# A first projection started by halves of the features, and identity products in TensorE's pauses

## The chip, the cores and the metric

One core of one Trainium2 chip. The time is device microseconds (us) for one execution of the whole program; of the kernel before there are three timed runs and one execution under the profiler.

## The reference

One step of a hybrid backbone with two layers, for 128 context tokens and 256 latent tokens of 1024 features, all in float32. Layer 0 mixes tokens by attention, layer 1 by a pooling over windows; each is followed by a mixture of 32 experts (two per token). Every sub-layer starts from a root-mean-square norm that is scaled and shifted by vectors made of the conditioning. Cut to what the change touches:

```python
def ada_modulation(cond, w, b):
    m = jax.nn.silu(cond) @ w + b            # 1024 -> 6 * 1024, per layer
    m = m.reshape(cond.shape[0], 1, N_MOD, D_MODEL)
    return tuple(m[:, :, i] for i in range(N_MOD))

def modulate(x, g, shift, scale):
    return rms_norm(x, g) * (1.0 + scale) + shift

for l in range(DEPTH):
    sh1, sc1, g1, sh2, sc2, g2 = ada_modulation(cond, ada_w[l], ada_b[l])
    h = modulate(x, norm_mix_g[l], sh1, sc1)
    m = attention(h @ w_qkv) @ w_o           # layer 0; pooling in layer 1
    x = x + g1 * m
    h = modulate(x, norm_ffn_g[l], sh2, sc2)
    x = x + g2 * hierarchical_moe(h, ...)
```

So the first product with `w_qkv` (1024 x 1536) needs `sh1` and `sc1`, which come from the first 2048 columns of `ada_w`.

## The kernel before

The program is written out by hand: each engine has its own list of instructions, in order, with waits on semaphores. Features lie on the 128 partitions in KD = 8 blocks k; tokens lie along the free axis, in three tiles of 128 (tile 0 is the context; `QTILES` = 1, 2, 0 is their order).

**The opening.** SyncE issues nearly all loads, in one order. `ada_w` comes in 24 chunks of 512 columns (2 MB each, `load_ada`, L409 to L411) into five places that are used in turn (`ADA_AT`); a chunk whose place was used before waits until TensorE has multiplied the earlier one (semaphore `ada_mm`). Chunks 0 and 1 hold the shift `sh1`, chunks 2 and 3 the scale `sc1`; the even one is for features 0 to 511, the odd one for 512 to 1023. The order of the loads is: constants, the tokens, chunks 0 to 3, two thirds of `w_qkv` (`load_qkv`, 2 MB each), chunk 4, the last third, chunks 5 and up.

TensorE (L1355 on) first makes the normed and turned tokens: 24 products of the tokens with `dg`, the identity scaled by the reciprocal root mean square (L1396), that VectorE copies to `hT` (`turned`, L908). Then, for chunks 0 to 3, `ada(i)` (L1374, eight products of 512 columns with 32 rows of output, four of them side by side in the array), with the transposes of the raw tokens between (`raw`, L1409; ScalarE copies them to `xT`, L694). `SETS` says which chunks share one bank: 0 to 3, 4 to 9, 10 to 23. When a set is complete, ScalarE copies it (`set_copy`, L689), `vectors` turns it into feature order (L1385), VectorE adds the bias, adds 1 and multiplies the gain (`modulation`, `scales`, L931 to L938), and scales and shifts `hT` block by block (L947, 16 operations). Only then the projection starts (L1449): nine groups g (three token tiles by three thirds of `w_qkv`), eight products each, into banks 5 to 7 in turn; between the groups stand `ada(4)` to `ada(11)` and the transposes for attention (`turn`, L1435). The other chunks are multiplied during attention (L1487 is its first product).

A product of float32 shows as two instructions in the trace, a transpose as one.

**A pass over the experts.** Per layer, 24 tiles of at most 64 gathered rows go through the experts' weights (3 MB per expert), which stream in through seven places for gate and up and six for down. Per tile: `gate_up` (L1748), `hidden_T` (a transpose, L1758), `down` (L1785). The last tile NS-1 has its own code: the gate and up product in two halves, `hidden_T`, and `down`, which waits until VectorE has copied the turned hidden rows (`hidT_ready`) and the last down weights have landed (`s_wout`). After it `second_result` (L1852) and `last_tile` (L1859) add the gathered results to the residual in PSUM, and VectorE writes the tokens (L1312, L1327). `busy(n, b)` (L1563) issues n products of the identity with itself into bank b, whose result nobody reads; the kernel before calls it with 7 once per layer, in the router.

## Time and profile before

| | |
|---|---|
| three runs | 765.98, 768.46, 769.75 us; median 768.46 us |
| profiled execution | 767.06 us, its span 765.2 us |
| TensorE busy | 646.9 us, 85% of the span |
| mean granted TensorE clock | 0.939 |
| VectorE, ScalarE, GpSimd busy | 39%, 17%, 16% |
| moved by DMA | 291.11 MB, mean 380 GB/s |

The profiled execution's 767.06 us is the span and 1.9 us around it; it lies 1.4 us under the median of the three. Busy shares are means over stages with different limits: the opening waits for loads, attention goes by TensorE, and in an expert pass the DMA engines never pause while TensorE does toward its end.

### The profile page before, as it was taken

How to read it: one execution, taken by the hardware profiler on the slowest of the kernel's cores; microseconds unless marked ns; L12 is line 12 of the kernel's file. 1: busy time of each engine (PE TensorE's matmuls, PEld its weight loads, DVE VectorE, ACT ScalarE, POOL GpSimd, SP SyncE). 2: the span in 40 equal slices, each digit the busy share in tenths (PEclk: the TensorE clock that was granted, in tenths of full speed). 3: DMA queues.
4: the chain of work that ended last, by engine and by line, in shares of the span. 5: the costliest groups of instructions: out<-in, count | busy, mean ns of one | idle time of the engine just before them, and what ended most of it. 6: DMA issues, size and time to landing. Idle time of an engine off the chain costs nothing.

```text
span 765.2 us, 12739 instructions
## 1 busy us (share of the span) xinstructions
PE 646.9 (85%) x4693; PEld 348.5 (46%) x4693; DVE 296.5 (39%) x721; ACT 132.4 (17%) x328; POOL 120.6 (16%) x194
## 2 busy tenths in 40 slices
PE   3899999999999999999844577899999997564685
PEld 3443343445796865554321232647655553222231
DVE  1215336765314644444221113666544443112123
ACT  3211134553116300000000000554000000000000
POOL 1000000001000033333312001010343333111010
PEclk9999999999999999999977689999999999777798
DMA  9999868949278799999999999999999999999996
GB/s 331 426 428 427 359 229 319 431 191 419 118 294 352 260 399 418 417 420 419 417 426 419 423 421 391 415 425 420 362 418 411 420 425 415 420 425 418 422 412 255
DMA packets 39577, 291.11 MB, mean 380 GB/s; under 512 B 7466, under 2 KB 8898, under 8 KB 20448
## 3 DMA queue, kind: packets, MB, share of 16 engines
q1 hardware_dynamic: 30112, 272.46, 86.2%
q0 software_dynamic: 7600, 12.81, 4.8%
q10 hardware_dynamic: 1808, 5.06, 1.7%
q8 instruction: 39, 0.64, 0.3%
q14 instruction: 18, 0.15, 0.0%
HBM read 284.68 MB, written 17.56 MB: 395 GB/s over the span
## 4 chain that ended last, share of the span: by engine, by line
PE 58%; DMA 26%; SPq 9%; DVE 4%; issue 2%; ACT 1%; DVEq 0%; POOLq 0%; POOL 0%
PE bank L1748 15%; PE bank L1449 8%; PE bank L1785 7%; DMA adas<-in_moe_w_in 6%; PE bank L1374 5%; DMA ring<-in_moe_w_in 4%; DMA cond_at<-in_moe_w_in 4%; PE bank L1548 4%; DMA ring<-in_ada_w 4%; DMA ring<-in_moe_w_out 4%; PE bank L1707 2%; PE bank L1556 2%; DMA adaw<-rows,gidx 2%; PE bank L1487 2%; PE bank L1508 2%
## 5 line engine op out<-in xcount | busy, mean ns | idle before, releaser
L1748 PE MATMUL bank<-ring,qkv 128*32 128x256 f32 (+1 forms) x1344 | 134.2, 423 | 39.4 <-DMA ring<-in_moe_w_in 25.0
L1748 PEld LDWEIGHTS bank<-ring,qkv 128*32 128x32 f32 (+1 forms) x1344 | 76.8, 133 | 82.4 <-issue 52.1
L1206 DVE COPY qkv<-bank 128x512 f32<-128x512 f32 x44 | 30.4, 691 | 200.8 <-PE bank L1707 200.8
L603 POOL DMA_INDIRECT results<-adaw,scur x46 | 47.2, 1026 | 249.9 <-DVE adaw L1229 216.3
L867 ACT ACTIVATE qkv<-bank 128x128 f32<-128x128 f32 x48 | 13.3, 277 | 408.5 <-PE bank L1748 408.5
L1785 PE MATMUL bank<-ring,qkv 128*32 128x512 f32 (+1 forms) x368 | 66.3, 609 | 4.6 <-DMA ring<-in_moe_w_out 4.6
L1449 PE MATMUL bank<-ring,hT 128*128 128x512 f32 x144 | 65.5, 610 | 1.3 <-DVE hT L947 1.3
L1748 PE MATMUL bank<-seventh,qkv 128*64 128x256 f32 (+1 forms) x224 | 35.5, 485 | 16.4 <-DMA ring<-in_moe_w_in 16.4
L593 POOL DMA_INDIRECT adaw<-rows,gcur x40 | 41.6, 1039 | 33.0 <-POOL gcur L590 27.8
L1449 PEld LDWEIGHTS bank<-ring,hT 128*128 128x128 f32 x144 | 27.3, 194 | 38.1 <-issue 36.9
L1748 PE MATMUL bank<-adaw,qkv 128*64 128x256 f32 (+1 forms) x256 | 36.6, 449 | 7.9 <-DMA adas<-in_moe_w_in 7.9
L1748 PE MATMUL bank<-xT,qkv 128*64 128x256 f32 (+1 forms) x192 | 30.9, 487 | 14.5 <-DMA cond_at<-in_moe_w_in 14.5
L1229 DVE SCALAR_TENSOR_TENSOR adaw<-bank,wcur,adaw 128x512 f32<-128x512 f32 x48 | 36.0, 751 | 10.2 <-PE bank L1785 8.7
L1226 DVE SCALAR_TENSOR_TENSOR adaw<-qkv,wcur 128x512 f32<-128x512 f32 x48 | 36.1, 752 | 1.7
L1218 DVE COPY qkv<-bank 128x128 f32<-128x128 f32 x48 | 14.0, 291 | 53.7 <-PE bank L1758 53.7
L736 ACT ACTIVATE ring<-bank,ss 128x384 f32<-128x384 f32 (+1 forms) x48 | 24.0, 505 | 34.8 <-DVE ss L1005 34.8
L1707 PE MATMUL bank<-con,adaw 128*128 128x128 f32 x176 | 28.9, 286 | 1.3 <-DMA adaw<-rows,gidx 1.3
L1785 PEld LDWEIGHTS bank<-ring,qkv 128*32 128x32 f32 (+1 forms) x368 | 15.9, 122 | 29.8 <-issue 29.6
L1748 PEld LDWEIGHTS bank<-seventh,qkv 128*64 128x64 f32 (+1 forms) x224 | 17.9, 152 | 25.0 <-issue 20.7
L1548 PE MATMUL bank<-hT,ring 128*128 128x256 f32 x128 | 29.1, 380 | 0.0
L1374 PE MATMUL bank<-ring,cond_at 128*32 128x512 f32 x224 | 26.9, 598 | 1.6 <-DMA ring<-in_ada_w 1.6
L1707 PEld LDWEIGHTS bank<-con,adaw 128*128 128x128 f32 x176 | 18.4, 140 | 19.7 <-issue 16.6
(260 smaller groups left out, 832.0 us busy)
## 6 DMA issues: line engine op xcount, KB each, us to landing
ring<-in_moe_w_in SPq DMA_DIRECT2D x37, 2048.0 KB, 19.9
ring<-in_moe_w_out SPq DMA_DIRECT2D x44, 1024.0 KB, 26.4
ring<-in_ada_w SPq DMA_DIRECT2D x14, 2048.0 KB, 14.8
adaw<-in_ada_w SPq DMA_DIRECT2D x10, 2048.0 KB, 15.2
adaw<-in_moe_w_in SPq DMA_DIRECT2D x8, 2048.0 KB, 22.6
seventh<-in_moe_w_in SPq DMA_DIRECT2D x8, 1792.0 KB, 24.9
xT<-in_moe_w_in SPq DMA_DIRECT2D x8, 1536.0 KB, 19.8
hT<-in_moe_w_out SPq DMA_DIRECT2D x10, 1024.0 KB, 25.4
```

The lines of the kernel that those rows point to most:

```text
L593: pool.indirect_dma_start(xg[:, b], None, rows, bass.IndirectOffsetOnAxis(ap=gcur[:, b:b + 1], axis=0), bounds_check=row_limit, oob_is_err ...
L603: pool.indirect_dma_start(res, bass.IndirectOffsetOnAxis(ap=scur[:, p, :], axis=0), yout[:, p], None, bounds_check=res_limit, oob_is_err=F ...
L736: last = A.activation(probs[:, u % 4, j, 0:nk], pairs[u % 2][:, j, 0:nk], ACT.Exp, bias=ss[:, 60 + 2 * (u % 2) + j:61 + 2 * (u % 2) + j], ...
L1206: V.tensor_copy(xgT[:, p], bank[2][:, :]).then_inc(xgT_ready, 1)
L1226: V.scalar_tensor_tensor(yout[:, p], gdiff, wcur[:, p, 1:2], glat, ALU.mult, ALU.add).then_inc(y_order, 1)
L1229: V.scalar_tensor_tensor(yout[:, p], bank[4 + p % 2][:, :], wcur[:, p, 0:1], yout[:, p], ALU.mult, ALU.mult)\
L1374: last = T.matmul(out[32 * j:32 * j + 32, :], condT[:, k, c:c + 32], w[:, k], start=i == SETS[n] and half == 0, stop=i + 1 == SETS[n + 1] ...
L1449: last = T.matmul(bank[5 + g % 3][:, :], hT[:, k, t * P:(t + 1) * P], wqkv[n][:, k, :], start=k == 0, stop=k == KD - 1)
L1548: last = T.matmul(bank[WO_BANKS[d % 2]][:, 0:NTOK - CTX], wo[:, k, d * P:(d + 1) * P], hT[:, k, CTX:NTOK], start=k == 0, stop=k == KD - 1)
L1707: last = T.transpose(bank[2][:, i * P:(i + 1) * P], xg[:, q, i * P:(i + 1) * P], ident)
L1748: last = T.matmul(bank[p][64 * a + m * h:64 * a + m * (h + 1), 0:2 * P], xk[:, k % 4, k // 4, m * h:m * (h + 1)], gate_up_of(b, k)[:, :, a ...
L1785: last = T.matmul(bank[4 + p][64 * a + m * h:64 * a + m * (h + 1), :], hidT[:, p, 64 * j + m * h:64 * j + m * (h + 1)], down_of(b, j)[:, a ...
```

## The change

It has two parts. **Part 1, the opening:** the set of chunks 0 to 3 becomes two sets, (0, 2) and (1, 3), each with shift and scale for one half of the features. The loads go by halves in that order: chunks 0 and 2, the first half of the rows of each third of `w_qkv` (1 MB each), chunks 1 and 3, the second halves. The tokens are only transposed (one instruction each), and normed by a VectorE multiplication with a row of reciprocals that `ones` times `dg` spreads to all partitions (`spread`, `normed`). The projection does features 0 to 511 for six groups, in six banks, with `ada(1)` and `ada(3)` between, then `vectors(1)`, then features 512 to 1023; groups 6 to 8 are done whole. 12 identity products (`warm`) stand around the first two chunks. ScalarE loads its square root's table before the tokens arrive. **Part 2:** in each expert pass 7 identity products stand before the last `down`.

Left out below: waits that count in the new numbering of sets, and the closures that only give a name to code that was there.

```diff
-        SETS = (0, 4, 10, 2 * NCH)
-        SET_BANK, VECTOR_BANK = (0, 1, 2), (2, 0, 2)
+        SETS = ((0, 2), (1, 3), tuple(range(4, 10)), tuple(range(10, 2 * NCH)))
+        SET_BANK, VECTOR_BANK = (0, 0, 1, 2), (2, 2, 0, 2)
+        HALF = KD // 2
+        QKV_BANKS = (1, 3, 4, 5, 6, 7, 5, 6, 7)
+        RAW_FIRST = (4, 5, 6)
+        SPREAD_BANKS = (7, 1, 2)
...
-            for i in range(4):
-                load_ada(i)
-            load_qkv(0)
-            load_qkv(1)
-            load_ada(4)
-            load_qkv(2)
-            for i in range(5, 2 * NCH):
+            def load_qkv(n, half):
+                if half:
+                    sp.wait_ge(s_wqkv[n], 16)
+                sp.dma_start(wqkv[n][:, half * HALF:(half + 1) * HALF].rearrange("p k n -> p (k n)"),
+                             attn_w_qkv[n][:, half * HALF * 512:(half + 1) * HALF * 512]).then_inc(s_wqkv[n], 16)
+
+            for half in range(2):
+                for i in SETS[half]:
+                    load_ada(i)
+                for n in range(3):
+                    load_qkv(n, half)
+            for i in range(4, 2 * NCH):
                 load_ada(i)
...
+            A.activation(ss[:, 7:8], C("eps"), ACT.Sqrt)
...
+            root_mean(0)
+            root_mean(1)
+            for n in range(4):
+                raw_copy(n)
+            root_mean(2)
+            raw_copy(4)
+            raw_copy(5)
             set_copy(0)
+            set_copy(1)
...
-            def turned(n):
-                dve.wait_ge(hn_mm, n + 1)
+            def normed(n):
                 t, q = QTILES[n // 2], n % 2
-                V.tensor_copy(hT[:, 4 * q:4 * q + 4, t * P:(t + 1) * P],
-                              bank[6 + n % 2][:, :].rearrange("p (k t) -> p k t", k=4)).then_inc(hn_copied, 1)
+                dve.wait_ge(hn_mm, n // 2 + 1)
+                dve.wait_ge(xt_copied, n + 1)
+                V.tensor_tensor(hT[:, 4 * q:4 * q + 4, t * P:(t + 1) * P], xT[:, 4 * q:4 * q + 4, t * P:(t + 1) * P],
+                                bank[SPREAD_BANKS[n // 2]][:, 0:P].unsqueeze(1).to_broadcast([P, HALF, P]), ALU.mult)\
+                    .then_inc(hn_copied, 1)
...
+            for half in range(2):
+                first = half * HALF
+                dve.wait_ge(ada_vec, half + 1)
...
+                for cond, a, b in reversed(CONDS):
+                    for k in range(first, first + HALF):
+                        V.tensor_scalar(hT[:, k, a:b], hT[:, k, a:b], mod(0, 1, k, cond), mod(0, 0, k, cond),
+                                        ALU.mult, ALU.add).then_inc(h_ready, 1)
...
+            def spread(n):
+                t = QTILES[n]
+                pe.wait_ge(dgx_ready, n + 1)
+                T.matmul(bank[SPREAD_BANKS[n]][:, 0:P], ones, dg[:, t], start=True, stop=True).then_inc(hn_mm, 1)
...
+            def warm(n, b):
+
+                for _ in range(n):
+                    T.matmul(bank[b][:, 0:P], ident, ident, start=True, stop=True)
+
+            ada(SETS[0][0])
+            pe.wait_ge(xt_copied, 6)
+            warm(7, 5)
+            ada(SETS[0][1])
+            pe.wait_ge(hn_copied, 6)
+            warm(2, 5)
             vectors(0)
+            warm(3, 5)
...
+            def product(g, half):
                 t, n = QTILES[g // 3], g % 3
-                pe.wait_ge(s_wqkv[n], 16)
-                if g >= 3:
-                    pe.wait_ge(qkv_sq, g - 2)
-                for k in range(KD):
+                pe.wait_ge(s_wqkv[n], 16 * half + 16)
+                for k in range(half * HALF, (half + 1) * HALF):
...
+            for g in range(6):
+                product(g, 0)
+                if g == 3:
+                    ada(1)
+                elif g == 4:
+                    ada(3)
+            vectors(1)
+            for g in range(9):
+                if g >= 6:
+                    pe.wait_ge(qkv_sq, g - 2)
+                    product(g, 0)
+                product(g, 1).then_inc(qkv_mm, 1)
...
                 hidden_T(NS - 1, (NS - 1) % 2)
+                busy(7, 5)
                 down(NS - 1, (NS - 1) % 2)
```

How the order on TensorE changes at the start of the projection (L1374 is `ada`, L1385 `vectors`, L1449 a product of the projection, L1409 `raw`), before:

```order
L1374 MATMUL bank<-adaw,cond_at 32x512 x8
L1409 MATMUL bank<-con,xtok 128x128 x8
L1374 MATMUL bank<-ring,cond_at 32x512 x8
L1385 MATMUL bank<-con,adas 128x4x2 x4
L1449 MATMUL bank<-ring,hT 128x512 x16
L1374 MATMUL bank<-ring,cond_at 32x512 x8
L1449 MATMUL bank<-ring,hT 128x512 x8
```

and in the change (there L1400 is `ada`, L1412 `vectors`, L1449 an identity product, L1490 a product of the projection):

```order
L1400 MATMUL bank<-ring,cond_at 32x512 x8
L1449 MATMUL bank<-con 128x128 x7
L1400 MATMUL bank<-adaw,cond_at 32x512 x8
L1449 MATMUL bank<-con 128x128 x2
L1412 MATMUL bank<-con,adas 128x2x2 x4
L1449 MATMUL bank<-con 128x128 x3
L1490 MATMUL bank<-ring,hT 128x512 x16
L1400 MATMUL bank<-adaw,cond_at 32x512 x8
L1490 MATMUL bank<-ring,hT 128x512 x4
L1400 MATMUL bank<-ring,cond_at 32x512 x8
L1490 MATMUL bank<-ring,hT 128x512 x4
L1412 MATMUL bank<-con,adas 128x2x2 x4
```

Two chunks stand ahead of the first product of the projection where four stood. The other two and a second `vectors` are now inside it, and the product behind that `vectors` waits for VectorE once more (`h_ready`).

SyncE's queue of loads in the opening of the change (L413 is `load_ada`, L449 `load_qkv`; the first two rows load the tokens):

```order
L443 DMA xtok<-in_x_sample 128x2x1024
L444 DMA xtok<-in_x_prompt 128x1024
L413 DMA ring<-in_ada_w 128x4096
L413 DMA adaw<-in_ada_w 128x4096
L449 DMA ring<-in_attn_w_qkv 128x2048 x3
L413 DMA adaw<-in_ada_w 128x4096
L413 DMA ring<-in_ada_w 128x4096
L449 DMA ring<-in_attn_w_qkv 128x2048 x3
L413 DMA ring<-in_ada_w 128x4096 x2
```

Before, the four chunks came first and nothing up to the last third of `w_qkv` waited; now each second half waits for its first to have landed, and the load of chunk 6 waits for the product with chunk 1, which comes later than before.

The end of pass 1 on TensorE in the change (L1804 is gate and up, L1763 a transpose of gathered rows, L1819 the residual, L1841 `down`, L1814 `hidden_T`, L1619 the identity products):

```order
L1804 MATMUL bank<-ring,qkv 32x256 x32
L1763 MATMUL bank<-con,adaw 128x128 x4
L1841 MATMUL bank<-ring,qkv 32x512 x8
L1814 MATMUL bank<-con,qkv 128x128
L1819 MATMUL bank<-xtok,con 128x512 x2
L1841 MATMUL bank<-hT,qkv 32x512 x4
...
L1804 MATMUL bank<-ring,qkv 32x256 x32
L1814 MATMUL bank<-con,qkv 128x128
L1619 MATMUL bank<-con 128x128 x7
L1841 MATMUL bank<-ring,qkv 32x512 x8
```

Before, the row with x7 was not there; all else at this place is the same.

## Rows read from the trace of the kernel before

**Rows 1.** The chain of waits in the opening: start us, us, what.

```profile
2.16 0.63 SPq L411
...
2.83 0.56 SPq L411
...
3.97 27.41 DMA ring<-in_ada_w
31.43 1.97 PE bank L1374 x16
33.42 0.60 ACT adas L689
34.07 1.07 PE bank L1385 x8
36.45 15.67 PE bank L1449 x32
52.12 1.85 PE bank L1374 x16
53.97 7.06 PE bank L1449 x16
...
118.76 1.49 PE bank L1487 x8
```

**Rows 2.** The DMA view: chunks 0 and 1, the last number us from issue to landing.

```profile
ring<-in_ada_w SPq DMA_DIRECT2D x1, 2048.0 KB, 14.0
...
adaw<-in_ada_w SPq DMA_DIRECT2D x1, 2048.0 KB, 18.2
```

**Rows 3.** Windows of 10 us: PE, PEld, DVE, ACT, POOL busy, granted clock, DMA share, GB/s.

```profile
100.00:110.00 10.00, 10.00 (x47) 4.76 (x46) 1.89 (x3) 3.42 (x9) 0.00 (x0) 1.00 0.56 228
...
430.00:440.00 10.00, 2.76 (x29) 1.44 (x29) 1.89 (x4) 0.00 (x0) 1.23 (x2) 0.64 1.02 426
```

**Rows 4.** Timeline, end of pass 1: start us, us, engine, line.

```profile
472.79 0.33 PE L1758 MATMUL bank<-con,qkv 128*128 128x128 f32 x1 [0.80 <-DVE qkv L1212]
475.39 1.92 PE L1785 MATMUL bank<-ring,qkv 128*32 128x512 f32 x16 [2.27 <-DMA ring<-in_moe_w_out]
```

**Rows 5.** The chain of waits at the end of pass 2.

```profile
749.13 2.56 PE bank L1785 x16
751.68 2.93 PE bank L1852 x4
754.62 2.78 PE bank L1859 x12
757.39 1.93 PE bank L1852 x4
```

**Rows 6.** Windows of 1 us there.

```profile
751.00:752.00 1.00, 1.00 (x5) 0.39 (x2) 0.20 (x1) 0.00 (x0) 0.00 (x0) 0.50 0.90 332
...
754.00:755.00 1.00, 1.00 (x4) 0.30 (x4) 0.00 (x0) 0.00 (x0) 0.00 (x0) 1.00 0.99 397
```

**Rows 7.** Timeline, ScalarE: squares of the three token tiles.

```profile
9.78 1.06 ACT L681 ACTIVATE qkv<-xtok 128x1024 f32<-128x1024 f32 x1 [3.65 <-DMA xtok<-in_x_sample]
...
12.44 1.04 ACT L681 ACTIVATE qkv<-xtok 128x1024 f32<-128x1024 f32 x1
...
13.80 1.04 ACT L681 ACTIVATE qkv<-xtok 128x1024 f32<-128x1024 f32 x1
```

**Rows 8.** Lines by form, 0 to 130 us: ScalarE's copies of the raw tokens.

```profile
L694 ACT ACTIVATE xT<-bank 128x512 f32<-128x512 f32 x6 | 3.3, 594 | 12.0 <-PE bank L1409 12.0
```

**Rows 9.** Windows of L1396 alone: TensorE's products, weight loads, clock, DMA.

```profile
14.00:14.50 0.50, 0.50 (x4) 0.50 (x4) 1.00 1.15 492
...
18.00:18.50 0.50, 0.50 (x7) 0.50 (x5) 1.00 1.07 459
```

**Rows 10.** A window of half a us early in the projection.

```profile
39.50:40.00 0.50, 0.50 (x2) 0.33 (x1) 0.50 (x3) 0.00 (x0) 0.00 (x0) 0.50 0.92 393
```

**Rows 11.** Timeline, end of pass 2: the last turn of the hidden rows.

```profile
746.48 0.33 PE L1758 MATMUL bank<-con,qkv 128*128 128x128 f32 x1 [0.80 <-DVE qkv L1212]
```

More of the change, by code:

```diff
@@ L1362, in ada @@
             def ada(i):
-                n = set_of(i)
-                c = 30 - 2 * (i - SETS[n])
+                n = [i in chunks for chunks in SETS].index(True)
+                c = 30 - 2 * SETS[n].index(i)
                 if i == 0:
@@ L1402, in _ @@
             T.transpose(bank[3][:, 64:160], rowsB[:, :], ident[0:96, 0:96]).then_inc(rows_mm, 1)
-            def raw(n):
-                t, q = n // 2, n % 2
-                if n >= 2:
-                    pe.wait_ge(xt_copied, n - 1)
-                for k in range(4):
-                    last = T.transpose(bank[4 + n % 2][:, k * P:(k + 1) * P],
-                                       xtok[:, t, (4 * q + k) * P:(4 * q + k + 1) * P], ident)
-                last.then_inc(xt_mm, 1)
-            for i in range(4):
-                ada(i)
-                if i < TT:
-                    raw(2 * i)
-                    raw(2 * i + 1)
+            spread(2)
+            def warm(n, b):
[7 more added lines that the diff above has]
+            warm(2, 5)
             vectors(0)
+            warm(3, 5)
             def turn(n):
@@ L1491, in _ @@
                 if u == 1:
-                    vectors(1)
+                    vectors(2)
                 if u in ADA_STEPS:
```

116 lines of the change are left out of this document (64 added, 52 removed).

## The prediction

> **What bounds the kernel now.** I read the chain of waits first, because it says which work a change must shorten, then the landing times, and then windows for the share of each engine where the chain changes hands. The chain starts as a chain of loads: the last of four chunks of the modulation weights is issued at 3.97 us and lands 27.41 us later, at 31.4 [rows 1]. Behind it stand the product with it (1.97), ScalarE's copy (0.60), the `vectors` (1.07) and VectorE, until the first product of the projection at 36.45 [rows 1]. From there to attention's first product at 118.76 the chain is TensorE alone: groups of 7.06 us with a chunk of 1.85 us between them [rows 1]. In that stretch the DMA engines are busy only 0.56 of the time [rows 3]: the loads wait for TensorE. Late in an expert pass it is the reverse: TensorE works 2.76 of 10 us and the DMA share is 1.02 [rows 3]. The stream of expert weights starts behind semaphores of TensorE (the last chunk's product, attention, the output projection), so a shorter opening should start the stream earlier and move the whole rest with it. At the very end four steps of TensorE are the chain [rows 5], two of them at a granted clock of 0.50, 1.2 GHz, and the third back at 2.4 GHz [rows 6].
>
> **Part 1, the start of the projection.** The loads are one stream. Chunk 0 is issued at 2.16 and lands after 14.0, at 16.2; chunk 1 is issued at 2.83 and lands after 18.2, at 21.0 [rows 1, 2]. That is 4.9 us for 2 MB. In the change chunk 2 has that second place, so the last load ahead of the first product lands at 21.0 and not at 31.4.
>
> TensorE may not be ready then. `ada(0)` now stands behind `spread` of the third tile. ScalarE squares the first tile at 9.78 and needs 1.36 us per tile (12.44 to 13.80) [rows 7], so two tiles are done at 12.5; four copies of 0.59 [rows 8] take it to 14.9, the third tile to 16.2; with VectorE's reciprocal and the `spread` itself, for which I take 1.1, `ada(0)` starts at 17.3, not 16.2. Its clock: the windows print 1.00 there, but the first products of the kernel pass at 4 in half a us and later at 7 [rows 9], so the engine began at 1.2 GHz and rose while it did products. I take all of `ada(0)` at 1.2 GHz, 3.7 us, to 21.0. An instruction of 512 columns takes 7.06/16 = 0.44 us at 2.4 GHz [rows 1], so an identity product (two instructions of 128 columns) takes an estimated 0.22 and seven take 1.5, to 22.5. `ada(2)` takes 1.97, to 24.5. From the end of the last chunk to the first product it was 36.45 - 33.40 = 3.05 us [rows 1]; the five identity products fit into that chain's two pauses. First product at 27.5, which is 8.95 us earlier. The bounds: 26.0 if TensorE is waiting when chunk 2 lands (21.0 + 1.97 + 3.05), and 30.9 if everything up to there goes at 1.2 GHz.
>
> Here a rule bears on which of these it is. The rows show the clock rising while TensorE did products with `dg` [rows 9]; the change does transposes in their place, and no row shows a rise during transposes alone. The Trainium skill (TensorE: Matmul & The Clock Gate, Part 4: PE-mode transpose) says that the full clock does not engage for transposes. By that rule `ada(0)` starts slow and the first product comes at 27.5; without it `ada(0)` would go at 2.4 GHz and the first product would come at 26.0. It speaks for the later value.
>
> **What is given back inside the projection.** The two chunks that stood ahead are now between groups: each costs 1.85 and 0.2 for the break (a group of 7.06 against 16 instructions of 0.43), together 4.1. A second `vectors` costs 1.07 and a break, 1.2 together. Behind it TensorE has nothing to do until VectorE has made the next `h`: before, that took 36.45 - (34.07 + 1.07) = 1.3 [rows 1], and the work is the same in kind. 6.6 us in all.
>
> **The clock at the start.** Early in the projection the granted clock was 0.50 [rows 10], after pauses of 0.6 and 1.3 us around `vectors`: two groups took 15.67 where two undisturbed ones take 13.9 [rows 1]. With the identity products in these pauses I take this 1.7 as gained. Sum of part 1: 8.95 + 1.7 - 6.6 = **4.1 us**; with the start at 26.0 it is 5.6, at 30.9 with the loss kept it is -1.0.
>
> **What covers the rest.** The transposes and norms of the opening lie beside loads. The first half of `w_qkv` lands in three pieces at 23.5, 25.9 and 28.4, and is wanted at 27.5, 30.9 and 34.4; chunk 1 lands at 33.3 for use at 41.2, chunk 3 at 38.2 for 46.7, the second halves at 40.6 to 45.6 for use from 54 on. All these waits are covered by 1.6 us or more. On SyncE the load of chunk 6 now waits for the product with chunk 1, at 43; but the queue ahead of it holds work until chunk 5 lands, at 21.0 + 7 x 4.9 = 55, so it costs nothing, and would cost only if that product came 12 us later. Freed later than that, all places follow TensorE as before.
>
> **Part 2, the ends of the passes.** In pass 2 the hidden rows are turned at 746.48 to 746.81 [rows 11] and the last `down` waits for its weights until 749.13 [rows 5]. Seven identity products take 1.5 of these 2.3 us, so they are free at 2.4 GHz. What they may bring is the clock: `down` took 2.56 and `second_result` 2.93 where at 2.4 GHz they take 1.92 and 1.93 [rows 4, 5], together **1.6 us**. In pass 1 the same pause (473.12 to 475.39) was followed by a `down` of 1.92 [rows 4], so nothing is to be won there and the products fit again. The bounds are 0 (the clock falls all the same, or VectorE then waits for results that are still landing) and 1.6. I take 1.6, since of the pause only two pieces are left, 0.8 ahead of the turn [rows 11] and 0.8 behind the seven products.
>
> **The sum.** 4.1 + 1.6 = 5.7 us. Against the profiled execution's 767.06 this is 761.4; against the median of the three runs, 1.4 us higher, it is 762.8. The three runs differ by 3.8, so I take the value between, 762.0.
>
> **The rivals.**
> - *A better opening:* the clock is up when chunk 0 is multiplied, the first product comes at 26.0, 1.5 us more: 760.5. The rows leave it open, the rule above speaks against it. 0.12.
> - *Only the opening:* the clock at the end of pass 2 falls all the same. 763.6. For it: the same pause led to a fall in pass 2 and not in pass 1, so more than its length decides. 0.13.
> - *Hidden anyway:* the opening's gain is lost in attention or in the passes, because chunks arrive late or because TensorE, whose clock is already down to 0.64 late in pass 1 [rows 3], is slow on a tile that is on the chain. Against it: the DMA share of 0.56 in the projection [rows 3]. For it: the tail of a pass has many short stretches of work at either clock. 4.1 us are lost, 766.1, or up to 768 if part 2 brings nothing. 0.14.
> - *The other side, identity products on a slow clock:* they do not raise it. Then the first product comes at 30.9, the 1.7 stay lost, and part 1 costs 1.0. At the ends of the passes seven products take 3.1 in a room of 2.3, 0.8 each. Together 2.6 slower, 771.1; if the new pause inside the projection lets the clock fall as well, 1.7 more, 772.8. It decides at one point: whether the granted clock is 0.50 when the product with chunk 2 starts. Against it: the clock rose in products of 128 columns [rows 9]. 0.06.
> - *The forecast:* 762.0, with 0.55.
>
> **How the numbers follow.** A measurement of this kernel can tell about 0.5% from no change, 3.8 us, so faster means under 764.6. The forecast and the two rivals next to it hold 0.80; the measurement's own spread puts about a tenth of that above 764.6, which leaves 0.72 for faster. Slower than 772.3 needs the last rival with its addition: 0.04. The rest, 0.24, is the same. The range reaches from the better opening with 3 us of spread, 757.5, to the middle of the hidden case, 767.5.
>
> **What would show it.** The first product of the projection at 27.5 (26.0 to 30.9) with the granted clock at 1.00; chunk 2 landing at 21.0; between features 0 to 511 and 512 to 1023 one pause of 1.3 us; attention's first product at 114.7 in place of 118.76; the same distance from there to the end of pass 1; at the end `down` near 1.9 and `second_result` near 1.9 at a clock of 1.00. I am wrong if the first product is on time and attention's first product is not (a wait inside the projection that I did not see), or if attention starts 4 us earlier and the end of pass 1 does not.

## The result, and the profile after

| | before | change |
|---|---|---|
| median, first comparison | 768.59 us (7 runs, 765.98 to 769.75) | **762.63 us** (7 runs, 759.2 to 763.72) |
| ratio | | 0.9914, 95% interval 0.989 to 0.9939 |
| median, repeated on another chip | 768.91 us (11 runs) | 762.69 us (6 runs), ratio 0.9912 (0.9893 to 0.993) |
| profiled execution, its span | 767.06 us, 765.2 us | 759.59 us, 757.5 us |

The change is faster by 6.0 and 6.2 us. The page of the change has this at its head (busy time of the engines, then the granted clock in 40 slices):

```profile
PE 647.5 (85%) x4711; PEld 349.6 (46%) x4711; DVE 297.0 (39%) x724; ACT 133.1 (18%) x330; POOL 120.6 (16%) x194
...
PEclk9999999999999999999966689999999999677799
```

TensorE's busy time is nearly that of before, 647.5 us against 646.9, but it now holds 26 more identity products, an estimated 6.4 us by the 1.73 that seven take below. So TensorE's other work takes some 6 us less, and part of its waiting is filled. The chain of waits in the opening of the change, which answers to [rows 1] (L1400 multiplies a chunk of modulation weights, L1449 are identity products, L1412 the `vectors`, L1490 the projection):

```profile
17.38 1.85 PE bank L1400 x16
19.24 1.76 PE bank L1449 x14
20.99 1.90 PE bank L1400 x16
...
23.57 1.07 PE bank L1412 x8
...
25.93 13.97 PE bank L1490 x32
39.90 1.85 PE bank L1400 x16
41.75 3.63 PE bank L1490 x8
45.38 1.85 PE bank L1400 x16
47.24 3.63 PE bank L1490 x8
50.87 0.80 PE bank L1412 x8
...
52.88 7.10 PE bank L1490 x16
```

The first product comes at 25.93 instead of 36.45, 10.5 us earlier, and the four half groups take 13.97 us instead of 15.67. The two chunks that moved behind it cost 1.85 each, the second `vectors` 0.80, and from 51.67 to 52.88 TensorE does nothing. Attention's first product comes at 112.82 in the timeline (before: 118.69; in the chains 112.89 and 118.76), 5.87 us earlier.

The ends of the two passes in the timeline of the change, for [rows 4, 5, 11] (L1814 turns the hidden rows, L1619 are the identity products, L1841 is the last `down`, L1909 `second_result`):

```profile
467.30 0.33 PE L1814 MATMUL bank<-con,qkv 128*128 128x128 f32 x1 [0.80 <-DVE qkv L1238]
467.47 1.73 PE L1619 MATMUL bank<-con 128*128 128x128 f32 x14
469.87 1.92 PE L1841 MATMUL bank<-ring,qkv 128*32 128x512 f32 x16 [0.68 <-DMA ring<-in_moe_w_out]
...
740.58 1.73 PE L1619 MATMUL bank<-con 128*128 128x128 f32 x14
743.07 1.92 PE L1841 MATMUL bank<-ring,qkv 128*32 128x512 f32 x16 [0.76 <-DMA ring<-in_moe_w_out]
744.92 1.98 PE L1909 MATMUL bank<-adaw,con 128*128 128x512 f32 x4
```

Of the pause of 2.3 us ahead of the last `down` there remain 0.68 and 0.76. Where the clock was at 0.50 [rows 6], it is at 1.00 (windows of 1 us, columns as in [rows 3]):

```profile
745.00:746.00 1.00, 1.00 (x3) 0.52 (x4) 0.75 (x1) 0.00 (x0) 0.00 (x0) 1.00 1.00 397
```

From attention's first product to the first gate and up product of pass 2 it is 413.95 us before and 414.23 after; from there to the last `down` of pass 2 216.49 and 216.02; from that `down` to the end of the span 16.07 and 14.43. So the spans' difference of 7.7 us is 5.87 at attention, -0.28, 0.47, and 1.64 at the end: in these two executions the rest of the program keeps its length within 0.5 us.

### The profile page after: what moved, and what is told of

It reads as the page before. It is cut to its first block, busy times and chain, and to the rows that moved or that the text cites. A ratio compares the mean times of both kernels' runs of the same rounds, so it can differ in the third digit from the quotient of the medians.

```text
span 757.5 us, 12788 instructions
## 1 busy us (share of the span) xinstructions
PE 647.5 (85%) x4711; PEld 349.6 (46%) x4711; DVE 297.0 (39%) x724; ACT 133.1 (18%) x330; POOL 120.6 (16%) x194
## 4 chain that ended last, share of the span: by engine, by line
PE 63%; DMA 25%; DVE 4%; SPq 4%; issue 2%; ACT 1%; DVEq 0%; POOLq 0%; POOL 0%
PE bank L1804 17%; DMA ring<-in_moe_w_in 9%; PE bank L1490 8%; PE bank L1841 8%; PE bank L1400 5%; DMA cond_at<-in_moe_w_in 4%; DMA ring<-in_moe_w_out 4%; PE bank L1604 4%; DMA adas<-in_moe_w_in 3%; PE bank L1763 2%; PE bank L1612 2%; DMA adaw<-rows,gidx 2%; PE bank L1543 2%; PE bank L1564 2%; PE bank L1708 2%
## 5 line engine op out<-in xcount | busy, mean ns | idle before, releaser
L1804 PE MATMUL bank<-ring,qkv 128*32 128x256 f32 (+1 forms) x1344 | 135.5, 428 | 38.5 <-DMA ring<-in_moe_w_in 25.8
L1804 PEld LDWEIGHTS bank<-ring,qkv 128*32 128x32 f32 (+1 forms) x1344 | 77.4, 134 | 82.3 <-issue 52.5
L1841 PE MATMUL bank<-ring,qkv 128*32 128x512 f32 (+1 forms) x368 | 65.7, 601 | 1.4 <-DMA ring<-in_moe_w_out 1.4
L1490 PE MATMUL bank<-ring,hT 128*128 128x512 f32 x144 | 64.6, 599 | 1.8 <-DVE hT L973 1.8
L1804 PE MATMUL bank<-seventh,qkv 128*64 128x256 f32 (+1 forms) x224 | 35.4, 483 | 16.7 <-DMA ring<-in_moe_w_in 16.7
L1490 PEld LDWEIGHTS bank<-ring,hT 128*128 128x128 f32 x144 | 26.5, 190 | 37.9 <-issue 35.2
L1804 PE MATMUL bank<-xT,qkv 128*64 128x256 f32 (+1 forms) x192 | 30.8, 486 | 14.4 <-DMA cond_at<-in_moe_w_in 14.4
L1804 PE MATMUL bank<-adaw,qkv 128*64 128x256 f32 (+1 forms) x256 | 36.4, 448 | 7.3 <-DMA adas<-in_moe_w_in 7.3
L1763 PE MATMUL bank<-con,adaw 128*128 128x128 f32 x176 | 28.8, 286 | 1.3 <-DMA adaw<-rows,gidx 1.3
L1804 PEld LDWEIGHTS bank<-seventh,qkv 128*64 128x64 f32 (+1 forms) x224 | 17.9, 151 | 25.1 <-issue 20.8
L1841 PEld LDWEIGHTS bank<-ring,qkv 128*32 128x32 f32 (+1 forms) x368 | 15.8, 122 | 26.6 <-issue 26.5
L1763 PEld LDWEIGHTS bank<-con,adaw 128*128 128x128 f32 x176 | 18.4, 140 | 19.7 <-issue 16.6
L1400 PE MATMUL bank<-ring,cond_at 128*32 128x512 f32 x224 | 26.9, 598 | 0.0
```

Of the source, the lines that this page charges most:

```text
L1400: last = T.matmul(out[32 * j:32 * j + 32, :], condT[:, k, c:c + 32], w[:, k], start=i == SETS[n][0] and half == 0, stop=i == SETS[n][-1] a ...
L1490: last = T.matmul(bank[QKV_BANKS[g]][:, :], hT[:, k, t * P:(t + 1) * P], wqkv[n][:, k, :], start=k == 0, stop=k == KD - 1, skip_group_chec ...
L1763: last = T.transpose(bank[2][:, i * P:(i + 1) * P], xg[:, q, i * P:(i + 1) * P], ident)
L1804: last = T.matmul(bank[p][64 * a + m * h:64 * a + m * (h + 1), 0:2 * P], xk[:, k % 4, k // 4, m * h:m * (h + 1)], gate_up_of(b, k)[:, :, a ...
L1841: last = T.matmul(bank[4 + p][64 * a + m * h:64 * a + m * (h + 1), :], hidT[:, p, 64 * j + m * h:64 * j + m * (h + 1)], down_of(b, j)[:, a ...
```

## The experiments

Each kernel is the change with one edit, unless it says otherwise. "Attention" is the start of attention's first product, "last down" that of the last `down` product. All times are of the profiled execution; medians and ratios are of the timed runs, each against the kernel before on the same chip. open_only_2, change_third and turns_alone were executed once each, so their times say little.

| kernel | median us | ratio (95%) | attention | last down, pass 1 | last down, pass 2 |
|---|---|---|---|---|---|
| before | 768.6 to 769.4 | | 118.69 | 475.39 | 749.13 |
| change | 762.63 | 0.9914 (0.989 to 0.9939) | 112.82 | 469.87 | 743.07 |
| change_again | 762.69 | 0.9912 (0.9893 to 0.993) | 114.55 | 471.22 | 747.17 |
| change_third | 762.35 (one run) | | 113.29 | 470.18 | 745.33 |
| open_only | 766.24 | 0.997 (0.9943 to 0.9997) | 113.22 | 469.85 | 748.60 |
| open_only_2 | 764.88 (one run) | | 113.07 | 469.97 | 745.63 |
| tail_only | 767.35 | 0.9969 (0.9947 to 0.9991) | 118.82 | 475.61 | 751.10 |
| no_warm | 764.5 | 0.9948 (0.9927 to 0.997) | 114.32 | 471.22 | 745.82 |
| whole_order | 766.18 | 0.9967 (0.9945 to 0.9989) | 118.01 | 474.78 | 748.69 |
| tail_14 | 763.58 | 0.9934 (0.9917 to 0.9952) | 114.50 | 472.56 | 745.92 |
| turns_alone | 771.47 (one run) | | 116.16 | 474.99 | 748.92 |
| vectors_early | 759.9 | 0.99 (0.9878 to 0.9923) | 111.45 | 468.30 | 742.03 |
| vectors_early_2 | 760.0 | 0.9891 (0.9868 to 0.9914) | 112.14 | 469.46 | 742.97 |
| filled | 760.74 | 0.9894 (0.9876 to 0.9913) | 111.53 | 468.38 | 743.45 |

### open_only: without the identity products at the ends of the passes

```diff
-                busy(7, 5)
                 down(NS - 1, (NS - 1) % 2)
```

> Theory: the opening carries nearly all of the gain. Attention's first product at 112.9 us as in the change, down of the last tile 5.9 to 6.1 us earlier than before; the clock may or may not fall at the end of pass 2, so the time lies 4.3 to 6 us under the kernel before, up to 1.6 us above the change. Rival (the identity products at the pass ends matter most): the time is within 3 us of the kernel before.

Attention came at 113.22, 0.4 later than in the change and 5.5 earlier than before. The time was missed: 4.3 to 6 us under the kernel before were expected, and the medians are 3.1 apart (2.3 by the ratio, 0.2 to 4.4 by its interval), about the rival's 3 us. The ratio of 0.997 has no overlap with the change's interval, so the identity products at the ends matter more than I had expected. At the end of pass 2 the fall was there as before the change. What I had not expected stood at the end of pass 1 (timeline):

```profile
469.85 3.54 PE L1841 MATMUL bank<-ring,qkv 128*32 128x512 f32 x16 [2.38 <-DMA ring<-in_moe_w_out]
476.53 3.68 PE L1908 MATMUL bank<-adaw,con 128*128 128x512 f32 x4 [3.14 <-issue]
```

The last `down` began when it does in the change and took 3.54 instead of 1.92, and after a pause of 3.14 us the next four instructions took 3.68 instead of 1.98. So the clock can fall at the end of pass 1 too. The pause itself is not the clock: behind the last `down` TensorE's queue has a branch that asks whether there are extra tiles, and here it took 6.19 us, from 470.0 on (the view of its line, durations in ns; in the change 0.47 us):

```profile
L338 PEldq COMPARE_BRANCH  x1: 6192/6192/6192, 470.0 to 470.0; - x1
```

### open_only_2: the same kernel, one more profiled execution

> A second look at the change without the identity products at the passes' ends. At the end of pass 1 its last look had the last down product at 3.54 and the second_result products at 3.68, at half clock, where the kernel before had 1.92 in both places. If that fall is a matter of the single execution, this one may show 1.92 there; if the shift of the pass by 6 us brought it, it is 3.5 again. At the end of pass 2 both theories have 2.56 to 2.8 for the last down product.

```profile
469.97 1.92 PE L1841 MATMUL bank<-ring,qkv 128*32 128x512 f32 x16 [2.25 <-DMA ring<-in_moe_w_out]
...
745.63 3.64 PE L1841 MATMUL bank<-ring,qkv 128*32 128x512 f32 x16 [2.31 <-DMA ring<-in_moe_w_out]
749.20 3.06 PE L1908 MATMUL bank<-adaw,con 128*128 128x512 f32 x4
```

With the same pause pass 1 now keeps the clock, and pass 2 loses 1.7 in `down` and 1.1 behind it. The fall belongs to the single execution and not to the code, and so does the long branch (0.48 us here).

### tail_only: the kernel before with `busy(7, 5)` at the ends of the passes

```diff
+                busy(7, 5)
                 down(NS - 1, (NS - 1) % 2)
```

> Theory: seven identity products before the last down cost nothing (they end at about 748.4, the weights come at 749.1) and keep the granted clock at 1.00, down 1.92 and second_result 1.93 us: 1.6 us under the profile of the kernel before, and 0 to 1.6 us less in the median, too little for the timing to tell. Rival (they delay down): 0.8 us slower per pass. Attention's first product stays at 118.7.

Both last `down` took 1.92 and `second_result` behind the second took 1.91. The median was 2.0 us lower (ratio 0.9947 to 0.9991), yet its profiled execution lasted 767.39, no less than 767.06 of the kernel before: pass 2 began at 535.32 instead of 532.64, 2.7 later. The traces say where: 0.2 at the last `down` of pass 1, 0.6 in a wait for the gathered results, and the rest at the window products of layer 1, here the kernel before and then tail_only:

```profile
486.58 1.19 PE L1877 MATMUL bank<-qkv,xtok 128*128 128x136 f32 x8 [1.79 <-DVE qkv L1306]
```

```profile
488.24 1.99 PE L1878 MATMUL bank<-qkv,xtok 128*128 128x136 f32 x8 [2.63 <-DVE qkv L1306]
```

The pause is 0.84 longer, and the slow clock behind it costs 1.0 up to the next large product. One profiled execution of each would have said that this part is worth nothing.

### no_warm: without the twelve identity products of the opening

```diff
             pe.wait_ge(xt_copied, 6)
-            warm(7, 5)
             ada(SETS[0][1])
             pe.wait_ge(hn_copied, 6)
-            warm(2, 5)
             vectors(0)
-            warm(3, 5)
```

> Theory: the twelve identity products of the opening keep the clock up. Without them TensorE is nearly idle from 19.2 to 25.9 except for the product with chunk 2, and the clock falls in the first products of the projection as it did before: attention's first product about 1.7 us later, 114.6, and the time 1.7 us above the change. Rival: the clock stays up without them (the pauses are shorter than before), attention at 112.9 and no difference.

```profile
17.70 1.92 PE L1400 MATMUL bank<-ring,cond_at 128*32 128x512 f32 x16
20.89 1.92 PE L1400 MATMUL bank<-adaw,cond_at 128*32 128x512 f32 x16 [1.26 <-DMA adaw<-in_ada_w]
...
25.94 15.46 PE L1487 MATMUL bank<-ring,hT 128*128 128x512 f32 x32 [1.31 <-DVE hT L973]
```

Without the identity products TensorE waits for chunk 2, rests 1.31 us ahead of the first product, and the same 32 instructions take 15.46 instead of 13.97. The first product comes at 25.94, as in the change, but `ada(0)` began 0.4 later than there. In open_only it began at the same time as here, with the identity products behind it:

```profile
17.71 1.92 PE L1400 MATMUL bank<-ring,cond_at 128*32 128x512 f32 x16
19.56 1.83 PE L1449 MATMUL bank<-con 128*128 128x128 f32 x14
21.32 1.93 PE L1400 MATMUL bank<-adaw,cond_at 128*32 128x512 f32 x16
```

There chunk 2 was multiplied at 21.32 instead of 20.89, and the first product came at 26.33. So the seven identity products delay it by 0.4 us where `ada(0)` begins that late, and they still pay. A window there (TensorE's products, weight loads, VectorE, ScalarE, GpSimd, clock, DMA share, GB/s):

```profile
26.00:27.00 1.00, 1.00 (x2) 0.48 (x3) 1.00 (x5) 0.00 (x0) 0.00 (x0) 0.50 1.08 451
```

Attention came 1.5 later, at 114.32, as the clock theory had it; the median is 1.9 us above the change's, with intervals that overlap.

### whole_order: four whole chunks and whole thirds of `w_qkv` again

The new norm and the identity products stay. Cut to its core:

```diff
-            for half in range(2):
-                for i in SETS[half]:
-                    load_ada(i)
-                for n in range(3):
-                    load_qkv(n, half)
+            for i in (0, 2, 1, 3):
+                load_ada(i)
+            load_qkv(0)
...
+            ada(1)
+            ada(3)
+            warm(2, 5)
+            pe.wait_ge(h_ready, 1)
+            vectors(1)
```

> The halves undone: all four chunks ahead of the projection, w_qkv in whole thirds, the new norm and the identity products kept. Theory: the halves bring most of the opening's gain. The fourth chunk lands at 31.4, the projection starts at 35.7 with the clock up, attention's first product at 116.3: only 2.5 us of the 5.9 are left, and the time is 3.4 us above the change. Rival (the new norm and the warm clock bring it): attention at 114 or earlier.

```profile
26.00 1.92 PE L1398 MATMUL bank<-adaw,cond_at 128*32 128x512 f32 x16 [0.94 <-DMA adaw<-in_ada_w]
31.54 3.57 PE L1398 MATMUL bank<-ring,cond_at 128*32 128x512 f32 x16 [3.62 <-DMA ring<-in_ada_w]
```

Attention came at 118.01, only 0.7 us earlier than in the kernel before and 1.7 later than expected. TensorE stands still for 3.62 us until the fourth chunk is there, and then multiplies it in 3.57 where the third took 1.92. No identity products stand in this wait. So the halves are what brings attention forward: 5.2 us against this kernel, of which 1.7 is this one fall. (This kernel keeps both `vectors`, and its first product, at 37.54, is 1.1 later than that of the kernel before.)

### change_again and change_third: the change itself, two more profiled executions

> The changed kernel once more, on the chip on which the next two stand and in as many rounds. By the theory that the halves bring 4.4 us at the attention's start, the opening's identity products 1.5 and those at the ends of the passes the rest, the ratio is 0.991 (0.989 to 0.994) as before, some 7 us under the kernel before; the profile has the attention's first product at 112.9 (before: 118.7) and both last down products at 1.92. If the earlier result was one chip's luck, the ratio is nearer to 0.996, as for each part alone.

```profile
25.97 15.67 PE L1490 MATMUL bank<-ring,hT 128*128 128x512 f32 x32 [0.54 <-DVE hT L973]
```

```profile
27.00:28.00 1.00, 1.00 (x2) 0.50 1.17 492
```

The first fence is its timeline, the second a window (TensorE's products, clock, DMA share, GB/s). The ratio held, the profile did not: with the same first product (25.97) and the same pause ahead of it (0.54) the clock fell to 0.50 here and attention came at 114.55, 1.7 later. My expectation of 112.9 was wrong.

> A third look at the changed kernel, for the pause at 25.4 and the one at 51.7. The first two looks had 13.97 and 15.67 us for the first four half groups and 7.10 both times for the two half products behind the second pause. Theory (a fall follows either pause in some executions): 13.97 or 15.67 and 7.10 or 8.80, the attention's first product at 112.8, 114.5 or 116.2, nothing between; the two last down products 1.92 in any case.

The first half groups took 13.97, the ones behind the second pause 7.10, and both last `down` 1.92 and 1.93, as expected; attention came at 113.29, which none of my three values was: the first product was itself at 26.40, 0.47 later, since chunk 2 landed at 21.3 instead of 20.7.

### tail_14: twice as many identity products at the ends

```diff
-                busy(7, 5)
+                busy(14, 5)
```

> Twice as many identity products ahead of each pass' last down product: 3.46 us instead of 1.73, where the changed kernel has 1.73 us of them and then 0.68 (pass 1) and 0.76 (pass 2) of waiting. Theory (they are harmless only as long as they fit into the wait, 2.4 us): the down product starts 1.05 later in pass 1 and 0.97 later in pass 2, both at 1.92, so the kernel is about 2 us slower than the change, or 1 us if pass 1 takes its part back in the wait for the scattered results. Rival (the number does not matter, the data sets the start): no difference.

```profile
52.86 8.80 PE L1490 MATMUL bank<-ring,hT 128*128 128x512 f32 x16 [1.21 <-DVE hT L973]
...
742.70 3.29 PE L1619 MATMUL bank<-con 128*128 128x128 f32 x28
745.92 1.92 PE L1841 MATMUL bank<-ring,qkv 128*32 128x512 f32 x16
```

From the turn of the hidden rows to the last `down` it is 3.39 us here in pass 2 and 4.12 in pass 1, against 2.65 and 2.57 in the change: 0.7 and 1.6 later. In pass 2 nothing is left of the wait. The median is 0.9 us above the change on the same chip, with intervals that overlap (0.9917 to 0.9952 and 0.9893 to 0.993), so the loss of 2 us is seen at its places in the trace and not settled in the time. In pass 1 the weights were also later, since 0.67 of waiting is left behind 28 instructions.

In the opening this execution shows one more fall, behind the 1.21 us in which TensorE waits for VectorE: 8.80 instead of 7.10.

### turns_alone: transposes and nothing else on TensorE

28 more transposes of the tokens, into a bank that is not read before it is written again:

```diff
             for n in range(3):
                 raw(n)
+            for _ in range(28):
+                T.transpose(bank[7][:, 0:P], xtok[:, 1, 0:P], ident)
             spread(0)
```

> 28 more transposes of the same rows of x into a bank nobody reads, ahead of the twelve identity products at 16.9 in the opening, and nothing but transposes on TensorE before them. In the changed kernel the first transposes are spaced 125 ns (x4 in 0.5 us at 10.0) and those at 14 to 15 about 70 ns apart (x7 in 0.5 us). Theory (transposes by themselves bring the clock up): the 28 run at the fast pace all along and the granted clock is 1.00 wherever they are, also for the first chunk's products behind them, 1.9 us. Rival (transposes do not count, only the two small products or the chance of the trace did): the pace goes back to the slow one in the course of the 28, and the first chunk's product takes about 3.7 us. The opening's products come 2 to 4 us later either way, so the time says nothing.

```profile
9.80 2.82 PE L1425 MATMUL bank<-con,xtok 128*128 128x128 f32 x12 [1.21 <-DMA xtok<-in_x_sample]
12.41 4.37 PE L1437 MATMUL bank<-con,xtok 128*128 128x128 f32 x28
...
17.06 1.47 PE L1425 MATMUL bank<-con,xtok 128*128 128x128 f32 x12
```

Windows of 1 us of the 28 alone (TensorE's products, weight loads, clock, DMA share, GB/s):

```profile
12.50:13.50 1.00, 1.00 (x6) 1.00 (x6) 1.00 0.92 393
...
14.50:15.50 1.00, 1.00 (x10) 1.00 (x9) 1.00 1.08 459
```

From 9.80 to 16.6 there are only transposes on TensorE. At first twelve of them take 2.82 us, later twelve take 1.47. Instructions overlap, so a window counts more than begin in it; from start to start it is 213 ns up to 14.76 and 109 ns behind it. The pace doubles in the middle of the 28, and the window prints a clock of 1.00 at both. (The 125 and 70 ns of my expectation were such counts, misread as spacings.) So transposes did bring the engine from 1.2 to 2.4 GHz, and both theories were off on the start: I had expected the fast pace for all 28. The Trainium skill (TensorE: Matmul & The Clock Gate, Part 4: PE-mode transpose) says that the full clock does not engage for them; this trace of float32 transposes disagrees. Whether transposes also keep a clock that something else raised is not told apart here.

The 771.47 us of this one execution are not the 28 transposes alone. They move attention to 116.16, 3.3 later than in the change, and behind the last `down` of pass 2 a branch takes 5.72 us, where it takes 0.22 in the change, so that TensorE pauses for 4.33.

This kernel has one more line that counts below, at the end of its pass 1, where the weights landed later:

```profile
474.99 3.15 PE L1843 MATMUL bank<-ring,qkv 128*32 128x512 f32 x16 [1.99 <-DMA ring<-in_moe_w_out]
```

### vectors_early: chunks 1 and 3 one group earlier, the second `vectors` ahead of the sixth half group

```diff
                 if g == 3:
                     ada(1)
+                    ada(3)
                 elif g == 4:
-                    ada(3)
-            vectors(1)
+                    vectors(1)
```

> Chunks 1 and 3 come one group earlier, so that VectorE fills the second `vectors` bank copy and its 1.2 us of modulation constants while TensorE is in the sixth group. In the changed kernel TensorE stands still 1.22 us there for hT (VectorE, L973). Theory (that pause is a plain wait on VectorE): it goes, the attention's first product comes at 111.7 instead of 112.9, and the kernel is 1.2 us faster than the change, ratio to the kernel before about 0.990. Rival one: chunks 1 and 3 have not landed that early (queue share 1.0 all along) and TensorE waits for them instead, 0 to 2 us, so that nothing is gained. Rival two: the pause moves into the seventh group, no gain.

> The order with chunks 1 and 3 one group earlier once more, beside the one above and on its chip. If its gain is real the ratio to the kernel before is again near 0.990 (0.988 to 0.992), 759 to 761 us; if it was one chip's luck it is that of the change, 0.991 and 762.6. Its profile has the attention's first product at 111.5, or at 113.2 where the clock falls after the pause at 25.4.

```profile
40.22 3.57 PE bank L1400 x32
43.79 3.63 PE bank L1490 x8
47.42 0.79 PE bank L1412 x8
48.21 10.41 PE bank L1490 x24
```

In the chain of waits both chunks follow each other without a wait for either, and behind the `vectors` the three half products run on at once: the pause is gone. Attention came at 111.45 and 112.14; the second is neither value expected, since its first product was at 26.93 and not at 26.25. From the first product to attention it is 85.2 in both, against 86.9 in the change. On one chip with change_again the median is 759.9 against 762.69, and the repeat gave 760.0. The traces account for 1.7 of these 2.8 us, 1.2 of it the pause; the other 1.1 may be falls that no longer follow the pause, which the medians alone don't prove, and the intervals of the ratios (0.9878 to 0.9923 and 0.9893 to 0.993) overlap. Of the versions that I ran it has, with `filled`, the lowest ratios.

### filled: vectors_early, with seven instead of three identity products ahead of the first product

```diff
-            warm(3, 5)
+            warm(7, 5)
```

> The last run's order (chunks 1 and 3 one group earlier, no pause behind the second vectors) and seven instead of three identity products behind the first vectors, so that TensorE is busy till VectorE's first tile of hT is there: x14 instead of x6 rows, some 0.5 us, in the 0.5 us of idle time at 25.4. Theory (each short pause of the opening is followed by a fall of the clock in some executions and not in others, and each fall costs 1.7 us: three repeats of one kernel had 13.97 us twice and 15.67 us once for the first four half groups): with that pause filled there is no fall before the attention, first four half groups at 13.97, attention's first product at 111.5 to 112.0, median 0 to 1 us under vectors_early. Rival (the falls have nothing to do with the pause): the median is as vectors_early or later by what the eight products overrun, 0.2 us, and falls still show.

```profile
24.75 1.81 PE L1449 MATMUL bank<-con 128*128 128x128 f32 x14
26.39 13.90 PE L1490 MATMUL bank<-ring,hT 128*128 128x512 f32 x32
```

No pause, no fall before attention, attention at 111.53; but the median of 760.74 is 0.7 above that of vectors_early_2 beside it. A pause of 0.54 was too seldom followed by a fall to be worth filling, as far as 6 runs can say.

### What the profiled executions have in common

The explanation that the runs led to: **a pause of TensorE is followed by a fall of the clock in some executions, seldom up to 1.8 us of pause and mostly from 2 us on.** I counted these pauses and looked whether the work behind each was at 0.50:

| pause of TensorE | kernels | its length, us | fell |
|---|---|---|---|
| ahead of the first product, no identity products there | before, tail_only, no_warm | 1.31 to 1.32 | 3 of 3 |
| ahead of the first chunk, behind transposes | all twelve executions with the new opening | 0.7 to 1.3 | 0 of 12 |
| ahead of a later chunk, no identity products in the pause | before and tail_only (fourth), no_warm (second), whole_order (third) | 0.9 to 1.6 | 0 of 4 |
| the same | whole_order, fourth chunk | 3.6 | 1 of 1 |
| ahead of the first product, identity products there | change (3 executions), open_only (2), tail_14, turns_alone, vectors_early (2) | 0.5 | 1 of 9 |
| behind the second `vectors` | change (3), open_only (2), no_warm, tail_14, turns_alone | 1.2 | 1 of 8 |
| last `down`, without identity products | before, open_only (2), both passes | 2.2 to 2.4 | 4 of 6 |
| last `down`, with them | all others, both passes | up to 0.8 | 0 of 21 |
| the same, weights late | turns_alone, pass 1 | 1.99 | 1 of 1 |
| behind a long branch at a pass' end | open_only pass 1, turns_alone pass 2 | 3.1 and 4.3 | 2 of 2 |
| window products behind pass 1 (136 columns), long | change_again, change_third, open_only_2, tail_only, filled, whole_order | 2.0 to 2.9 | 5 of 6 |
| the same, short | before, change, open_only, no_warm, tail_14, turns_alone, vectors_early (2) | 1.3 to 1.8 | 0 of 8 |

Two rows of the window products, a short pause and a long one, from the change and from change_third (timelines):

```profile
481.00 1.19 PE L1934 MATMUL bank<-qkv,xtok 128*128 128x136 f32 x8 [1.73 <-DVE qkv L1332]
```

```profile
481.64 2.14 PE L1934 MATMUL bank<-qkv,xtok 128*128 128x136 f32 x8 [2.07 <-DVE qkv L1332]
```

From here to the next large product (384 columns) it is 7.97 us in the change and 9.01 in change_third. Length of the one pause is not all: 1.31 fell three times of three, and 1.3 to 1.8 elsewhere never. Two more pauses stand close ahead of each of those three: in the kernel before 1.64 at 31.43 and 0.72 at 34.07, in no_warm 1.26 at 20.89 and 0.80 at 23.61. So what the identity products of the opening take away is a row of three pauses, and which of the three fillings counts was not tested. Without the first line of the table 2 of 62 pauses of up to 1.8 us were followed by a fall, and 13 of 16 from 1.99 us on. (Not counted are the pauses of under 1 us within the passes, one of about 1.5 early in attention, and the waits of 3.5 to 8.3 us for weights late in pass 1, where the clock falls again and again, 0.64 in [rows 3].)

## Why the prediction was right, and where its steps were not

**The time.** 762.0 us were forecast with 757.5 to 767.5, and 762.63 measured. The gain against the median of before was forecast as 6.5 and measured as 6.0. The total is right partly because misses cancel, and that is luck: in the profiled executions attention comes 5.87 earlier and not 4.1, and the end of pass 2 gives 1.6 as forecast, yet the median gains 6.0. For part 1 alone 4.1 were forecast and 3.1 measured (open_only, 0.2 to 4.4 by its interval); part 2 brought more than its 1.6 by the medians.

**The mechanism of part 1 holds.** Two chunks ahead of the first product instead of four, the rest beside it. whole_order shows it by its absence: attention at 118.01.

**The step that failed: "I take all of `ada(0)` at 1.2 GHz, 3.7 us, to 21.0".** It took 1.85, at 17.38 as foreseen (17.3). The clock was up by then: the first twelve transposes took 2.82 us and the second twelve 1.51, and the windows count 4 and 7 in half a us (the change, TensorE alone):

```profile
10.00:10.50 0.50, 0.50 (x4) 1.00 1.05 439
14.00:14.50 0.50, 0.50 (x7) 1.00 1.07 459
```

Two products with `dg` stand between them here; turns_alone shows that transposes suffice. The seven identity products took 1.76 and not 1.5, `ada(2)` began at 20.99 and took 1.90, and from its end to the first product it was 3.04 against 3.05: the first product came at 25.93, not at 27.5. The bound of 26.0 is the right number, but not for its reason. Chunk 2 had landed at 20.7 and TensorE was not waiting for it; the two times happened to lie 0.2 apart. Over the executions with the new opening `ada(0)` began between 16.8 and 18.3 (turns_alone apart), and where it began late the first product came later than the landing asked for (26.33 in open_only, 26.93 in vectors_early_2). The rule of the Trainium skill that I let speak for the later value (TensorE: Matmul & The Clock Gate, Part 4: PE-mode transpose) misled here; turns_alone disagrees with it too. The rival "better opening" had this start, and a total of 760.5 with it.

**Given back inside the projection: right.** From the first product to attention it is 82.31 before and 86.96 in the change, 4.65 more; with the 1.70 of the clock that is 6.35 against 6.6 forecast. The second `vectors` cost 0.80 and not 1.07 with a break; the pause was 1.22 against 1.3, and vectors_early shows that it was avoidable.

**The clock at the start: right in the profiled execution, too certain otherwise.** The 1.7 is there, and no_warm gives 1.5 of it back. But change_again lost it again behind a pause of 0.54, and tail_14 behind 1.21. "I take this 1.7 as gained" should have been a chance, since the five identity products leave half a us open and a new pause of 1.2 was part of the sum. That may be why the better start did not end at 760.5: a profiled 759.59 stands in a set of runs from 759.2 to 763.72.

**The cover: right.** No chunk and no half of `w_qkv` was waited for by TensorE behind the first product. SyncE's load of chunk 6 did wait for the product with chunk 1 and was issued at 41.82, 14.6 us before chunk 5 landed (56.4), so the queue never ran empty by it. The "1.6 us or more" of cover was less than the forecast's own times give (4.0 at the least, 23.5 against 27.5); measured, the first half of `w_qkv` lands 2.7 ahead of its use.

**Part 2: right in pass 2, wrong in pass 1.** "So nothing is to be won there" was read from one execution in which the clock happened to hold. open_only lost 1.6 in `down` there, and 1.7 in `second_result` behind the long branch, open_only_2 neither. Part 2 is a matter of chance in both passes: the change without it has a ratio of 0.997, with it 0.9914 and 0.9912; alone it has 0.9969. Against 1.6 us forecast the medians say 3.6 us inside the change (766.24 against 762.63, not on one chip) and 2.0 alone, each with an uncertainty of 2 to 3. How much of the 3.6 is long branches that happened to fall into open_only's runs stays open.

**The rivals.** "Only the opening" (the clock at the end falls all the same) did not happen: 0 falls of 21 with the identity products and a short wait. "Hidden anyway" did not either in the profiled execution: the distance from attention to pass 2 grew by 0.28. In the time it is not quite excluded, since open_only is 5.5 us ahead at attention and 3.1 in the median. "Identity products on a slow clock" is out, since the clock was up at the first of them, and at its point of decision, when chunk 2 was multiplied, the product took 1.92 or 1.93 in all three executions of the change.

**What stays open.** What decides in which execution a pause is followed by a fall. The Trainium skill (TensorE: Matmul & The Clock Gate, Part 1: The HAM clock gate) says that the chip's look at TensorE's activity runs freely and doesn't start with the kernel, so that one kernel measures differently from run to run; the scatter of the table agrees with that, and so does the rise in the opening (the second twelve transposes took 2.51 us in open_only and 1.62 in open_only_2, from the same code), but no run here tests it. Open is also why the pauses ahead of the window products differ (1.79 and 2.63 us on VectorE in the kernel before and tail_only, which makes most of the 2.7 us between their passes 2), and why a branch at the end of a pass took 6.19, 5.72 and 1.85 us three times (open_only, turns_alone, tail_14), where all others in these traces take 0.2 to 0.5; no run here tests either.

## What to carry to other kernels

Where the first product waits for a row of loads, ask for which part of the sum each load is needed, and start with the part whose loads are complete; then look what the second part's preparation leaves as a new pause, and put it under a product. A pause of TensorE can cost more than its length, by up to about 1.7 us here, but only in some executions: fill it with products that nobody reads when the room is certain (seven of them delayed the first product by 0.4 us where it was not), and judge such an edit by medians of several runs, because one profiled execution may show either. A term taken from one execution of a clock that falls by chance belongs into the range and not into the sum.

## What the runs showed of the hardware

- Transposes raise the clock: with nothing else on TensorE their spacing went from 213 to 109 ns (turns_alone, at 14.76). The granted clock in the windows printed 1.00 at either pace, so early in a kernel the pace has to be read from the instructions.
- Identical code with an identical pause (0.54 us) had the granted clock at 1.00 in one execution and at 0.50 in another. The fall cost 1.7 us in a stretch that TensorE fills (15.67 against 13.97, 8.80 against 7.10), and 1.0 where part of the slow stretch lies in waits.
- A branch on TensorE's queue that mostly takes 0.2 to 0.5 us took 6.19 us once in open_only and 5.72 once in turns_alone, and TensorE paused 3.14 and 4.33 us for it. With it and the two falls at that place pass 2 began at 533.18 in open_only and at 528.78 in open_only_2, from last `down` products that began 0.12 apart, though open_only_2 lost 2 us at the window products.
- One profiled execution can hold such an event or not; the count of pauses above has falls of the clock 2 times in 62 for pauses of up to 1.8 us and 13 times in 16 from 1.99 us on, the row of three pauses in the opening apart.
